# Two transformer layers in one kernel: norms moved off GpSimd, their sums of squares into the stage before, two units of weights taken k tile by k tile, and the first loads reordered

## What is computed

```python
for l in range(2):
    m, mc = adaln(silu(c), w_mod[l], b_mod[l]), adaln(silu(c_ctx), w_mod[l], b_mod[l])   # 9 vectors of 1024 each
    x  = x  + 0.5 * m[2]  * swiglu(modulate(rmsnorm(x,  norm_w[l, 0]), m[0],  m[1]),  ffn1_w13[l], ffn1_w2[l])
    xc = xc + 0.5 * mc[2] * swiglu(modulate(rmsnorm(xc, norm_w[l, 0]), mc[0], mc[1]), ffn1_w13[l], ffn1_w2[l])
    h, hc = modulate(rmsnorm(x, norm_w[l, 1]), m[3], m[4]), modulate(rmsnorm(xc, norm_w[l, 1]), mc[3], mc[4])
    y, yc = mixer(h, hc, ...)        # window attention and gated linear attention, merged, then w_out
    x = x + m[5] * y                 # and xc alike, in layer 0
    x = x + 0.5 * m[8] * swiglu(modulate(rmsnorm(x, norm_w[l, 2]), m[6], m[7]), ffn2_w13[l], ffn2_w2[l])
# rmsnorm(x, w) = x * rsqrt(mean(x^2) + eps) * w;   modulate(h, shift, scale) = h * (1 + scale) + shift
```

## Time and profile before

| what | value |
|---|---|
| median of 3 runs | 2698.78 us (2697.11 to 2700.98) |
| the profiled execution | 2704.55 us, of which its span is 2702.8 us |
| PE busy | 90% of the span |
| DVE / ACT / POOL busy | 40% / 32% / 9% |
| mean granted TensorE clock | 0.95 |
| read from HBM | 299 MB |

### The profile page before, as it was taken

One profiled execution on the slowest core, in us unless ns is written; L12 is line 12 of the kernel. 1 busy time (PEld: TensorE's weight loads), 2 busy tenths in 40 slices (PEclk: granted clock), 3 DMA queues, 4 the chain that ended last, 5 costly groups with the idle time before them and its releaser, 6 DMA issues.

```text
span 2702.8 us, 29281 instructions
## 1 busy us (share of the span) xinstructions
PE 2427.4 (90%) x12529; PEld 1976.6 (73%) x12529; DVE 1088.5 (40%) x1444; ACT 871.4 (32%) x1216; POOL 253.1 (9%) x296
## 2 busy tenths in 40 slices
PE   4999999878987878889999989999989797888998
PEld 2777777656876766767777857777868696778998
DVE  2323222465245453343323242232245635555553
ACT  2222222344234442232222132222124434444442
POOL 1000000100025350010000010000010005320000
PEclk7999999889999998989999989999999898989999
DMA  6555422210321111225453325654223042224564
GB/s 222 184 192 182 156 91 80 63 32 21 105 64 46 47 48 61 79 76 162 152 156 117 102 81 185 198 176 140 93 64 94 29 144 63 63 70 149 161 183 141
DMA packets 290185, 302.04 MB, mean 112 GB/s; under 512 B 6496, under 2 KB 267592, under 8 KB 281864
## 3 DMA queue, kind: packets, MB, share of 16 engines
q1 hardware_dynamic: 290056, 300.18, 34.7%
HBM read 299.10 MB, written 1.05 MB: 111 GB/s over the span
## 4 chain that ended last, share of the span: by engine, by line
PE 76%; DVE 10%; issue 6%; ACT 4%; POOL 3%; DMA 1%; SPq 0%; DVEq 0%; POOLq 0%; ACTq 0%
PE PS L1150 22%; PE PS L1151 22%; PE PS L1152 22%; PE PS L1200 3%; DVE sq L833 2%; PE PS L1458 1%; PE PS L1235 1%; POOL dq L473 1%; DVE hL L826 1%; DMA mraw<-in_w_mod 1%; DVE WL L776 1%; PE PS L1419 1%; DVE small L941 1%; ACT dq L685 1%; POOL dq L488 1%
## 5 line engine op out<-in xcount | busy, mean ns | idle before, releaser
L1150 PE MATMUL PS<-hH,WH 128*128 128x512 f32 (+1 forms) x2096 | 777.7, 371 | 48.3 <-DVE hL L826 34.2
L1152 PE MATMUL PS<-hH,WL 128*128 128x512 f32 (+1 forms) x2096 | 756.7, 361 | 0.0
L1151 PE MATMUL PS<-hL,WH 128*128 128x512 f32 (+1 forms) x2096 | 756.6, 361 | 0.0
L776 DVE TENSOR_TENSOR WL<-raw,WH 128x1024 fp32r<-128x1024 f32 x420 | 502.7, 1238 | 531.4 <-ACT WH L516 530.7
L516 ACT CAST WH<-raw 128x1024 fp32r<-128x1024 f32 x420 | 418.9, 1046 | 457.2 <-PE PS L1152 417.3
L1150 PEld LDWEIGHTS PS<-hH,WH 128*128 128x128 f32 x2096 | 402.3, 192 | 172.7 <-issue 85.0
L1152 PEld LDWEIGHTS PS<-hH,WL 128*128 128x128 f32 x2096 | 402.4, 192 | 60.0
L1151 PEld LDWEIGHTS PS<-hL,WH 128*128 128x128 f32 x2096 | 403.5, 192 | 53.9 <-issue 1.0
L1150 PE MATMUL PS<-hidH,WH 128*128 128x512 f32 (+1 forms) x704 | 257.5, 366 | 11.3 <-issue 10.4
L1151 PE MATMUL PS<-hidL,WH 128*128 128x512 f32 (+1 forms) x704 | 257.3, 365 | 0.0
L1152 PE MATMUL PS<-hidH,WL 128*128 128x512 f32 (+1 forms) x704 | 257.0, 365 | 0.0
(11 more groups left out here) (170 smaller groups left out, 2564.0 us busy)
## 6 DMA issues: line engine op xcount, KB each, us to landing
raw<-in_ffn_w SPq DMA_DIRECT2D x176, 512.0 KB, 5.1
mraw<-in_w_mod SPq DMA_DIRECT2D x64, 1024.0 KB, 7.8
raw<-in_w_in SPq DMA_DIRECT2D x54, 1024.0 KB, 5.2
raw<-in_ffn_w SPq DMA_DIRECT2D x44, 1024.0 KB, 4.9
raw<-in_w_branch_attn SPq DMA_DIRECT2D x8, 1024.0 KB, 4.9
raw<-in_w_branch_gla SPq DMA_DIRECT2D x8, 1024.0 KB, 4.9
raw<-in_w_out SPq DMA_DIRECT2D x8, 1024.0 KB, 4.9
mraw<-in_w_mod SPq DMA_DIRECT2D x16, 512.0 KB, 6.6
```

The costliest lines, as they stand in the source:

```text
L776: nc.vector.tensor_tensor(half(WL, n % 2, e, rows), half(raw, n % 2, e, rows), half(WH, n % 2, e, rows).bitcast(F32), ALU.subtract).then_i ...
L1150: mm(o, wh, ah, start=start, stop=False)
L1151: mm(o, wh, al, start=False, stop=False)
L1152: return mm(o, wl, ah, start=False, stop=stop)
```

## The change

1. **Norms without POOL.** POOL's product and DVE's scale and shift become one DVE operation on 256 columns, `xT * coefA * rstd` (a `scalar_tensor_tensor`, twice for each k tile). The shift is added by ACT as the bias of the rounding to `hH` (two halves), and again by DVE in the operation that makes `hL` (two halves).
2. **Sums of squares inside the last chunk.** In the last FFN chunk, PE does the sum of squares of k tile m-2 behind output tile m; in `out_proj`, two of them behind each unit from the second on. Two tiles remain for the end. ACT's squares in `out_proj` move in between its `prep`s.
3. **First two units k tile by k tile** (`first_two`). For k tiles 0 to 3, PE does both units' part of a k tile before the next; then k tiles 4 to 7 of the first unit, then those of the second. The second unit's `prep` moves ahead of the norm's end: its first half ahead of the last square, its second half behind it. The `adaln` pieces at places 0 to 3 now all stand behind the two units.
4. **First loads.** SP loads `x` and `ctx` first; set 0's eight `w_mod` pieces have buffers of their own and wait for nothing; the first two units' weights are loaded in the middle of them; the constants come last. ACT issues the small loads. DVE makes `WL` of both first units ahead of the `adaln` vectors.

```diff
@@ buffers and first loads
+            mfirst_b = sb("mfirst_b", [P, 4, MW], stack=r)
+            mfirst_a = sb("mfirst_a", [P, 2, MW], stack=r)
...
+            sp.dma_start(xin[:, 0:2, :], a["x"][0].rearrange("(t p) d -> p t d", p=P)).then_inc(x_in, 16)
+            sp.dma_start(xin[:, 2:4, :], a["ctx"][0].rearrange("(t p) d -> p t d", p=P)).then_inc(x_in, 16)
...
-                if p >= 2:
+                if p >= KT:
                     sp.wait_ge(mod_mm, p - 1)
...
+            for p in range(4):
+                load_mod(p)
+            for f in range(2):
+                load_pair(START[("ffn_in", 0)] + f, f, w13_d[0])
+            for p in range(4, KT):
+                load_mod(p)
@@ POOL
-            def norm(n, T):
-                pool.wait_ge(rstd_done, n + 1)
-                for kt in range(KT):
-                    nc.gpsimd.tensor_tensor(sq[:, kt, 0:T], xT[:, kt, 0:T], rstd[:, 0:T], ALU.mult).then_inc(xn_done, 1)
@@ ACT, norm
+                for kt in range(KT - 2 if j == 2 else 0, KT):
+                    if n and kt == KT - 1:
+                        prep(second, only=0)
+                    square(n, kt, T)
+                if n:
+                    prep(second, only=1)
                 act.wait_ge(ss_done, n + 1)
...
                 for kt in range(KT):
-                    act.wait_ge(hf_done, KT * n + kt + 1)
-                    nc.scalar.copy(hH[:, kt, 0:T], sq[:, kt, 0:T]).then_inc(h_hi, 1)
+                    act.wait_ge(xn_done, KT * n + kt + 1)
+                    for c in range(T // S):
+                        shift = mod[:, (N_MOD * l + 3 * j) * KT + kt, c:c + 1]
+                        ins = nc.scalar.activation(hH[:, kt, c * S:(c + 1) * S], sq[:, kt, c * S:(c + 1) * S], ACT.Identity, bias=shift)
+                    ins.then_inc(h_hi, 1)
@@ DVE, norm
+                    for c in range(T // S):
+                        own = slice(c * S, (c + 1) * S)
+                        ins = nc.vector.scalar_tensor_tensor(hL[:, kt, own], sq[:, kt, own], shift[:, kt, c:c + 1],
+                                                             hH[:, kt, own].bitcast(F32), ALU.add, ALU.subtract)
+                    ins.then_inc(h_ready, 1)
+
+                if n:
+                    prep(next_units(n)[1])
+                dve.wait_ge(rstd_done, n + 1)
                 for kt in range(KT):
-                    dve.wait_ge(xn_done, KT * n + kt + 1)
                     for c in range(T // S):
-                        ins = nc.vector.tensor_scalar(sq[:, kt, c * S:(c + 1) * S], sq[:, kt, c * S:(c + 1) * S],
-                                                      coefA[:, kt, c:c + 1], shift[:, kt, c:c + 1], ALU.mult, ALU.add)
+                        own = slice(c * S, (c + 1) * S)
+                        ins = nc.vector.scalar_tensor_tensor(sq[:, kt, own], xT[:, kt, own], coefA[:, kt, c:c + 1], rstd[:, own],
+                                                             ALU.mult, ALU.mult)
@@ PE
+            def first_two(norm, first, second):
+
+                n = next_units(norm)[0]
+                pe.wait_ge(lo_ready, 2 * n + 2)
+                for kt in range(KT // 2):
+                    pe.wait_ge(h_ready, KT * norm + kt + 1)
+                    first(n, kt)
+                    if kt == 0:
+                        pe.wait_ge(lo_ready, 2 * n + 4)
+                    second(n + 1, kt)
+                for kt in range(KT // 2, KT):
+                    pe.wait_ge(h_ready, KT * norm + kt + 1)
+                    first(n, kt)
+                for kt in range(KT // 2, KT):
+                    second(n + 1, kt)
...
-                for f in range(FT):
-                    if f > 1:
-                        pe.wait_ge((gated_a, gated_b)[f % 2], g0 + f // 2)
-                    unit_cols(n + f, 2 + f % 2, hH, hL, T, step=-2, h0=KT * ffn_norm(k) if f == 0 else None,
+                first_two(ffn_norm(k), lambda u, kt: cols_step(u, kt, 2, T, -2), lambda u, kt: cols_step(u, kt, 3, T, -2))
+                for at in range(4):
+                    mods_at(at)
...
+                            if f == FT - 1 and k < 3 and m > 1:
+                                squares_sum(ffn_norm(k) + 1, m - 2, T)
```

More of the change, by code:

```diff
@@ L175, in hybrid_backbone @@
         const_in = sem("const_in")
+        ones_in = sem("ones_in")
+        mfirst_in = [sem(f"mfirst_in{i}") for i in range(KT)]
         x_in = sem("x_in")
@@ L514, in prep @@
                     act.wait_ge(gate_in[f], 16 * count)
-                for e in range(2):
+                for e in range(2) if only is None else (only,):
                     nc.scalar.copy(half(WH, n % 2, e, rows), half(raw, n % 2, e, rows)).then_inc(hi_ready, 1)
@@ L749, in out_proj @@
                     prep(n + j + 1)
+                    if j:
+                        for kt in (2 * j - 2, 2 * j - 1):
+                            square(3 * l + 2, kt, tokens(2 * l + 1))
             for l in range(DEPTH):
@@ L1155, in weights, with unit_cols @@
                 return (WH[:, par, :].rearrange("p (k c) -> p k c", k=KT), WL[:, par, :].rearrange("p (k c) -> p k c", k=KT))
-            def unit_cols(n, bank, rh, rl, T, tiles=2, step=1, between=None, h0=None):
+            def unit_cols(n, bank, rh, rl, T, tiles=2, step=1, between=None):
                 wh, wl = weights(n % 2)
@@ L1179, in unit_rows @@
                     for kt in range(KT):
-                        if h0 is not None and b == 0:
-                            pe.wait_ge(h_ready, h0 + kt + 1)
                         ah, al = hH[:, kt, b * P:(b + 1) * P], hL[:, kt, b * P:(b + 1) * P]
@@ L1231, in _, with squares_sum @@
                 ins.then_inc(x_t, 1)
-            def norm(n, T):
-                for kt in range(KT):
-                    pe.wait_ge(sq_done, KT * n + kt + 1)
-                    ins = mm(PS[:, 0, 0:T], ones[:], sq[:, kt, 0:T], start=kt == 0, stop=kt == KT - 1)
-                ins.then_inc(ss_done, 1)
-            pe.wait_ge(const_in, 16 * 5)
-            norm(0, T2)
+            def squares_sum(n, kt, T):
+                pe.wait_ge(sq_done, KT * n + kt + 1)
+                ins = mm(PS[:, 0, 0:T], ones[:], sq[:, kt, 0:T], start=kt == 0, stop=kt == KT - 1)
+                if kt == KT - 1:
+                    ins.then_inc(ss_done, 1)
+            pe.wait_ge(ones_in, 16)
+            for kt in range(KT):
+                squares_sum(0, kt, T2)
             pe.wait_ge(x_ready, KT)
@@ L1489, in out_proj @@
                     unit_cols(n + j, 2 * j, actH, actL, T)
+                    if j:
+                        squares_sum(3 * l + 2, 2 * j - 2, T)
+                        squares_sum(3 * l + 2, 2 * j - 1, T)
+                for kt in range(KT - 2, KT):
+                    squares_sum(3 * l + 2, kt, T)
             for l in range(DEPTH):
-                if l:
-                    norm(3 * l, T2)
                 ffn(2 * l)
-                norm(3 * l + 1, T2)
                 attn_proj(l)
```

146 lines of the change are left out of this document (84 added, 62 removed).

## The result

The changed kernel takes 2655.22 us (median of 4 runs, 2647.94 to 2656.89), before 2698.65 on the same chip. The ratio is 0.9833, with a 95% interval of 0.9813 to 0.9853: 1.7% faster. The forecast was faster and 2640, with a range of 2622 to 2660, so the time lies in the range, 15 us behind the point and 5 us from the upper end. The profiled execution took 2647.94, the fastest of the four.

The account below looks back on a forecast made before the run. PE, busy 90% of the span, bounds the kernel, with its longest idle times at the norms and the start. Gains of 46.5 and 23.6 less 11 make 59.1 us, taking the 2698.8 median to 2640; range 2622 to 2660.

Parts of the forecast that it names:

- The new wait of 3.8: In FFN 0 and 2, PE waits 3.8 us for the third piece's load; with the clock's fall, 5.5 twice, 11 lost.
- The sums in the last chunk: Sums of squares end later: 0.8 us at norms 1, 3 and 4, 1.1 at norm 2, 1.4 at norm 5.
- The prediction's 2749: Rival: changing PSUM banks holds PE at 1.2 GHz throughout the two units, 109 us lost; slower cases together 0.02.
- this rival: DVE stays at 1.27 us per operation, 32 taking 41 us at each norm; no chance beyond the slow case's 0.02.
- The last chunk waits: Rival: sums stall the last chunk, about 8 us in each of three chunks, time 2664; chance 0.05.
- The first loads: Rival: first loads miss the DMA's pace, last piece at 45 in place of 35.5, time 2650; chance 0.10.
- The start: Last piece at 35.5, first FFN matmul at 42.4, two units done at 68.8 for 92.40: 23.6 us gained.
- The clock: After PE's wait at each norm the clock stands low at first, costing 1.7 us.
- The chain to the first matmul: At the norms, PE starts 4.0 us after the sums of squares end, 5.7 earlier than before.
- The two units: First two units k tile by k tile: PE never waits for h after the first k tile and needs 21.8 us.
- The stretches over attention and GLA: Stretches from two units to the next norm's Ln: forecast change +1.1 us in layer 0, +1.4 in layer 1.
- the 59.1: Total saving over the whole kernel: 46.5 at the norms and 23.6 at the start, less 11 for the new wait.

Follow-up runs that it names:

- experiment 5: Changed kernel with the old order of first loads on SP and two buffers for the w_mod pieces: 2673.42 us, ratio 0.989 to before.
- experiment 6: Changed kernel with PE taking the first unit, then the second, as before the change: 2678.03 us, ratio 0.9905 to before.
- experiment 7: Changed kernel with the norm's arithmetic as before, product with rstd on POOL: 2674.11 us, ratio 0.9889 to before.
- experiment 2: Changed kernel with the pieces at places 2 and 3 moved into the middle of an FFN stage's third unit: 2640.57 us, ratio 0.978 to before.
- experiment 3: Changed kernel with four unread matmuls on PE in the wait of norms 1 to 5: 2638.49 us, ratio 0.9771 to before.
- repeated pair of profiles: Second profiles of both kernels, each run again unchanged: changed 2655.81 us, before 2698.87 us; profiled spans 2655.6 and 2697.1.
- experiment 8: Changed kernel with the piece at place 3 moved, sums behind the last tile, unread matmuls at norms 1 to 5 and FFN 0 to 2 second halves: 2618.97 us.
- experiment 10: The kernel of experiment 8 run again unchanged, on another chip: 2616.23 us, ratio 0.9695 to before.

## Why the prediction was right, and where it was off

**The mechanism.** Each step shows in the trace, and experiments 5, 6 and 7 take three of them out one by one: the loads 21 us at the start, the two units k tile by k tile 27, the arithmetic without POOL 25, of which the FFN stages give back 5 and 2. By the ratios of the medians the three are 14, 18 and 14 us, each with some 6 us of uncertainty; in the profiles, what is missing lies in the attention and GLA stretches and at norm 5. The shorter chain and the k tiles nearly add up: norms 1 to 5 took 181.1 us before and 131.9 after, 155.0 with the shorter chain alone (experiment 6) and 155.9 with the k tiles alone (experiment 7); 4.8 us of each gain are the two pairs of pieces that moved out of norms 2 and 3 into the FFN stages. The new wait of 3.8 measured 4.38 and 4.18, and with its clock it cost 11.9 (experiment 2) for a forecast of 11. The sums in the last chunk are a small loss, as forecast: 0.95 for 0.8 per FFN norm. (The working there gives 7.5 against 7.0, so 0.5, and takes 0.8.)

**The rivals.** PE stayed at 1.00 over long stretches with bank changes after every 3 matmuls: in experiment 3, norm 2 with both units. The Trainium skill ("TensorE: Matmul & The Clock Gate", "A second HAM failure mode: psum-queue depth-cycling") reports a clock that swings for bf16 matmuls of N=512 that cycle through the banks. In this loop, with operands rounded to fp32r, it did not swing once the wait ahead of it was filled: 1.00 over the 26.4 us of that window. The prediction's 2749 is for the low clock throughout, so a swing between the two levels would have given less than that. DVE's product had 0.42, near the residual's 0.40, and not 1.27. The trace of before could have ruled this rival out, since its own scale and shift falls to 0.36 per operation where POOL is done; the rows are in the last section. The last chunk waits 0.34 for a square once. The first loads were late by 2.3 us, not by 9: of the rivals' times the 2650 of this one is nearest to the 2655, but not for its reason.

**Where the 15 us went.** No step of the mechanism failed; terms of the sum were mis-sized, nearly all in one direction. In the repeated pair of profiles 17.6 us are missing: 2.6 at the start, 4.4 at norms 1 to 4, 2.6 at norm 5, 3.9 in FFN 0 to 2 and 3.9 in the stretches over attention and GLA, with 0.1 at the end.
- *The start*, 2.6: the last piece started at 37.8 for 35.5. `x` and `ctx` had landed at 9.6, where the sum has them at 8.4; the FFN weights took 7.1 us for 6.4, and the last four pieces 11.1, 2.8 each for 2.5. Against that, the 1.0 kept for the constants wasn't needed, since they landed behind the last piece. The chain from the last piece to the first matmul was 0.3 longer than forecast.
- *The clock*, priced at 1.7 for each norm. Keeping it up gave back 1.5, 2.8, 2.1, 1.5 and 1.5 to 2.5 (experiment 3). The wait at the start of the FFNs' second half, which the change doesn't touch, also costs more now. In FFN 0 it is 3.46 us in both kernels, but in the changed one the clock falls 1 us ahead of the next matmul and stays at 0.50 until 331.8:

```profile
326.01 0.77 PE L1179 MATMUL PS<-hidH,WH 128*128 128x512 f32 x1 [3.46 <-issue]
```

```profile
325.00:331.70 6.70, 5.69 (x14) 4.48 (x15) 3.17 (x4) 1.44 (x2) 0.00 (x0) 0.50 0.31 115
```

  where before it stood low for 3.4 us. I take half of PE's busy time at the low clock as its cost, an estimate from these rows: 1.7 us before, 2.9 now. FFN 1 and 2 are alike, 6.8 us low for 3.4. The sum has nothing for these three. In experiments 8 and 10, with this, the piece's wait and the place of the sums removed, FFN 0 and 2 lie below the changed kernel by 9.2 and 9.9.
- *The chain to the first matmul*: 4.3 for 4.0 at norms 1 to 4, and 3.0 for 2.3 at norm 5, whose 2.3 the prediction doesn't work out.
- *The two units*: 21.8 was taken for all norms, but at norms 1 and 4 the first unit is 96 matmuls of 128x256, one per 0.119 us: 11.4 for 10.9. With the clock at 1.00 these two units took 22.8 from the first matmul to `qsq` (experiment 3).
- *The stretches over attention and GLA*: +1.1 and +1.4 forecast, +2.3 and +4.1 in the pair of repeated profiles, but -1.0 and -5.6 in the first pair. They move by several us from execution to execution, so that two profiles don't show how much of this part is the change's.
- *The base*: the sum was made against a profiled execution that was 5.8 us over its median, and its excess lay in such a stretch. A saving taken from its norms was right there. But the profiled execution of the changed kernel then lay 7 us under its own median, so the first pair of profiles differs by 56.6 us, close to the 59.1, and hides that the medians differ by 43.4. That first agreement is luck.

**What stays open.** How far the change moves the attention and GLA stretches on average: two profiles of each kernel don't tell 2 us from chance. Whether the clock could be kept up in the attention and GLA stretches, where experiment 8 still has it at 0.50 for 150 us in all, wasn't tried. The early `prep` of the second unit and the small loads on ACT were in every experiment, so what each of them is worth isn't shown.

## What to carry to other kernels

When a chain between two stages of matmuls can't be made shorter, give PE more work per piece that the chain delivers: here 12 matmuls or more per k tile in place of 3 hid a producer of 1.58 us per k tile, and it was worth as much as the shorter chain. When work is regrouped, follow the loads that reuse a buffer: three pieces put together cost 12 us that spreading them gave back. Where PE waited 3 to 5 us here, a few matmuls that nobody reads were cheaper than the fall of the clock. Two profiles of one kernel should be compared stretch by stretch before a sum of some ten us is believed.

## What the runs showed of the hardware

- PE's wait of 4.3 us with the clock at 1.00 was followed by a fall after PE had started again: at norm 1 of the changed kernel the matmuls start at 460.76 with a pace of 0.12, and go to 0.21 at 461.6. Here matmuls paid for a wait that was over. A wait of one length cost different amounts: 1.7 us before and 2.9 after for the same 3.46 us in FFN 0.
- Matmuls with an unread result (3.6 us of them in a wait of 4.3) kept the clock at 1.00 at all five norms (experiment 3), and three more in each wait of 3.5 us did so in FFN 0, 1 and 2 (experiment 8). At norm 1 the first matmul with `h` still came 4.30 us behind the sums.
- DVE was slower while POOL worked beside it. In the kernel before, POOL's last product of norm 1 ends at 482.2. The same scale and shift takes DVE 1.31 us per operation up to there and 0.36 behind it, the same difference `hL` 1.75 and 0.68:

```profile
471.70 10.50 POOL L464 TENSOR_TENSOR sq<-xT,rstd 128x512 f32<-128x512 f32 x8 [430.80 <-ACT rstd L533]
478.06 1.75 DVE L826 TENSOR_TENSOR hL<-sq,hH 128x512 fp32r<-128x512 f32 x1
479.73 2.62 DVE L833 TENSOR_SCALAR sq<-sq,coefA,mod 128x256 f32<-128x256 f32 x2
482.28 0.68 DVE L826 TENSOR_TENSOR hL<-sq,hH 128x512 fp32r<-128x512 f32 x1
482.88 0.72 DVE L833 TENSOR_SCALAR sq<-sq,coefA,mod 128x256 f32<-128x256 f32 x2
```

- The order of the large loads held: in the changed kernel `x`, `ctx`, the eight pieces and the four weight loads between them landed one after another in the order of the queue, the first at 6.7 us, the last at 37.7. But SP's own issue took up to 10.39 us for one load while earlier ones were under way:

```profile
5.55 10.39 SPq L380 DMA_DIRECT2D raw<-in_ffn_w  x1
```

  The DMA stayed busy meanwhile, at 415 to 429 GB/s in windows of 3 us from 6 to 18.
